# A two-layer attention trunk on one core: a narrower last head, a last head kept on chip, a new entry order

## Chip, cores and metric

The kernel runs as one program on one core of one Trainium2 chip. The metric is the device time of one execution in microseconds (us), median of several runs. Engines are named as in the profile: PE is TensorE (matmuls; PEld is its weight load, which overlaps PE), DVE is VectorE, ACT is ScalarE, POOL is GpSimd, SP is the SyncE queue that issues most transfers.

## What is computed

Two layers on 1024 tokens of width 1024 in float32. Each layer is attention, a residual layer norm, a gated feed-forward part with a width-3 convolution, and again a residual layer norm.

```python
x = layer_norm(alpha * x + mix, ln_g[i, 0], ln_b[i, 0])
ff = conv_ffn(x, ffn_w_in[i], ...)
x = layer_norm(alpha * x + ff, ln_g[i, 1], ln_b[i, 1])

# layer 0: differential attention, 8 heads of 128 columns, two maps per head
a = p[:, :, 0] - lam * p[:, :, 1]          # p = softmax(q k^T - slope * |t - s|)
o = rms_norm(a @ v, subln_g) * (1 - lambda_init);  mix = o @ w_o

# layer 1: neighbourhood attention, 16 heads of 64, grid of 16 rows x 64 columns
s = q_row . k_sel + bias                   # 8 x 16 window around each query
p = softmax(s);  o = p @ v_sel;  mix = o @ w_o + b_o
```

## The kernel before

Every large product is made of three matmuls on rounded parts: a float32 operand is split into a high part (rounded copy, by ACT or POOL) and a low part (operand minus high, by DVE or POOL), and high x high, high x low and low x high are summed in PSUM. `XTh` and `XTl` hold the two parts of the activations, turned, in eight slots of 128x1024; `raw_weights` holds two incoming weight tiles.

The program is a row of stages, each with its own semaphores; at the end of each all engines meet at a barrier and POOL clears the semaphores (line 43): differential attention (prefix `da`), output product with layer norm (`wo`), feed-forward (`ff`), neighbourhood attention (`na`), again `wo`, again `ff`. There is no planner: each engine's list is written out by hand, and semaphores alone tie the lists together.

**Entry (`da`).** PE turns x, then projects head 0: six groups `project(0, j, ...)` of 24 matmuls, in the order of `ORDER`. PE then starts `head(0)`, whose first act is `project(1, 0, 0, 10)`, followed by `score(0, 0)`. `project(1, 0)` needs the split weights of head 1 (`split(1, 0)` on POOL, lines 318 and 320) and all six takes of the projections by ACT (line 595); `score` needs the stacked keys: `KH` and `QS` from ACT (lines 657, 658), their low parts and a copy of `KL` from DVE (lines 758, 761, 764), and a copy of `KH` from POOL (`double_k`, line 344). After these, POOL splits head 1's other weights and only then scales the first map (line 326).

**Last head of `da` and the first `wo`.** Heads 0 and 1 are loaded back and split while the last head runs (`FirstHeads`). The last head's four output pieces go DVE (line 747), `ostage`, SP (line 259), DRAM tensor `heads_t`. The stage ends when the last store has landed. `wo` begins with ACT making the high part of the output weights' row tile 0 (line 1142), DVE its low part (line 1160), then PE's first products (line 1111); heads 2 to 7 are loaded from `heads_t` on the way.

**Neighbourhood attention (`na`).** A head is of 16 steps s (two halves c of 8 query tiles). In a step PE makes the scores of s (lines 2220 to 2227), turns the map of s-2 (line 2236) and weighs the values with the map of s-4 (lines 2264, 2270); between these stand projections of the next head, except in the last head, which has none. DVE adds the bias and takes the minimum (2449), makes the low part of the map (2401), inverts the sum (2459); ACT takes the exponential (2375) and the high part (2328); POOL scales (2108). `V` as the stationary operand holds high and low values side by side (128 columns), the moving operand holds the map's high and low parts side by side, so one matmul of 256 columns gives four partial sums: two in the two halves of the columns, two in the two halves of the partitions. Every second step ACT copies the lower 64 partitions (2343, 64x512), DVE adds them to the upper ones (2415, 64x512) and then adds the two column halves (2422, 64x256) into `ostage`, which SP stores. A query tile whose two grid rows have different windows ("wraps", steps 2 to 5 and 10 to 13) has three matmuls of 256 columns and two of 128 (2 x 64).

**The end.** In the last `ff`, after the last products, DVE handles the eight row tiles t in turn: two adds out of PSUM with sums (1909), mean (977), gain (995), variance (1000), and for t of 4 and more also the last step of the norm, `finish` (1007), one tile behind, with tile 7 at the very end. `finish` needs POOL's root (930). POOL also shifts tiles 0 to 3 (942). SP stores each finished tile of 512 KB (1375).

## Time and profile before

| | |
|---|---|
| median of 3 runs | 2799.16 us (lowest 2797.43) |
| the profiled execution's own time | 2802.47 us |
| its span in the trace | 2800.5 us |
| PE busy | 2658.3 us (95%), 13043 matmuls |
| DVE busy | 1927.1 us (69%) |
| POOL busy | 1671.4 us (60%) |
| ACT busy | 1191.7 us (43%) |
| mean granted PE clock | 0.978 of full |

Busy times are of the whole span. "Idle before" in a row is the engine's idle time just ahead of that instruction, and what follows the arrow is what ended it. PEclk is the clock granted to TensorE: 1.00 is 2.4 GHz and 0.50 is 1.2 GHz. The span and the execution's own time differ by 2.0 us, which lie outside the instructions.

### The profile page before, as it was taken

Reading aid. Unit: us, or ns where it says so; the run is one execution under the profiler, and the core shown is the slowest. Engines: PE = TensorE matmul, PEld = TensorE weight load, DVE = VectorE, ACT = ScalarE, POOL = GpSimd, SP = SyncE. Lnnn points to the kernel's source line nnn. Section 1 sums busy time; section 2 is a strip of 40 time slices with the busy share of each in tenths; the row PEclk is TensorE's granted clock in tenths of the full one; section 3 lists DMA queues with packets and bytes.
Section 4 is the critical chain, followed back from the end, with each engine's and each line's share of the span. In section 5 each row is a group of like instructions: output and inputs, shape, how many; then the busy total and the mean of one; then the engine's idle time right before and its main releaser. Section 6 shows DMA issues by size and latency. Waiting matters only on the chain. (4 is left out here: it accounts for less than half of the span.)

```text
span 2800.5 us, 35855 instructions
## 1 busy us (share of the span) xinstructions
PE 2658.3 (95%) x13043; PEld 2220.2 (79%) x13043; DVE 1927.1 (69%) x2479; ACT 1191.7 (43%) x1785; POOL 1671.4 (60%) x1179
## 2 busy tenths in 40 slices
PE   8999999988899999999989999998788999999998
PEld 6788888877778888888868888887677888888886
DVE  3766667683677766677774777777477777666768
ACT  3455444552253333333344555555415333333333
POOL 4444444333487667777744666655457776677775
PEclk9999999998999999999999999998899999999999
DMA  3010000235011112121222212211411211121212
GB/s 121 21 31 30 30 28 22 64 94 186 15 56 46 46 61 60 46 61 46 63 95 54 56 48 50 47 46 53 156 39 55 60 46 46 59 62 46 60 46 91
DMA packets 214044, 163.83 MB, mean 58 GB/s; under 512 B 36283, under 2 KB 195595, under 8 KB 213899
## 3 DMA queue, kind: packets, MB, share of 16 engines
q1 hardware_dynamic: 213755, 161.38, 19.5%
q8 instruction: 89, 1.46, 0.2%
q10 hardware_dynamic: 144, 0.52, 0.1%
q14 instruction: 56, 0.46, 0.1%
HBM read 137.24 MB, written 24.64 MB: 58 GB/s over the span
## 5 line engine op out<-in xcount | busy, mean ns | idle before, releaser
L1400 POOL TENSOR_TENSOR ff_Rlf<-raw_weights 128x512 f32<-128x512 f32 x210 | 330.6, 1587 | 53.4 <-PE ff_ph L1497 32.6
L1407 POOL TENSOR_TENSOR ff_Rl<-ff_Rlf,ff_Rh 128x512 fp32r<-128x512 f32 x210 | 310.7, 1496 | 25.2 <-ACT ff_Rh L1663 25.2
L1407 POOL TENSOR_TENSOR ff_Rl<-raw_weights,ff_Rh 128x512 fp32r<-128x512 f32 x84 | 157.8, 1888 | 253.5 <-ACT ff_Rh L1663 253.5
L1663 ACT ACTIVATE ff_Rh<-ff_Rlf 128x512 fp32r<-128x512 f32 x210 | 130.5, 630 | 366.6 <-POOL ff_Rlf L1400 366.4
L1497 PE MATMUL ff_ph<-XTh,ff_Rh 128*128 128x512 f32 x672 | 263.2, 392 | 8.7 <-POOL ff_Rl L1407 8.4
L1497 PE MATMUL ff_ph<-XTl,ff_Rh 128*128 128x512 f32 x672 | 262.2, 390 | 0.0
L1497 PE MATMUL ff_ph<-XTh,ff_Rl 128*128 128x512 f32 x672 | 262.1, 390 | 0.0
L1544 PE MATMUL ff_po<-ff_WDh,WH 128*128 128x512 f32 x624 | 244.5, 392 | 0.0
L1544 PE MATMUL ff_po<-ff_WDh,WL 128*128 128x512 f32 x624 | 243.0, 389 | 0.0
L1544 PE MATMUL ff_po<-ff_WDl,WH 128*128 128x512 f32 x624 | 242.9, 389 | 0.0
L1765 DVE TENSOR_TENSOR X<-ff_po,X 128x512 f32<-128x512 f32 x288 | 191.4, 684 | 66.0 <-PE ff_po L1544 66.0
L2108 POOL TENSOR_SCALAR na_E<-na_E,na_rden 128x512 f32<-128x512 f32 x128 | 104.7, 818 | 194.1 <-DVE na_rden L2459 193.5
L689 ACT ACTIVATE da_E<-da_S,da_mn 128x1024 f32<-128x1024 f32 x112 | 125.1, 1117 | 196.4 <-DVE da_mn L769 195.9
L1497 PE MATMUL ff_ph<-WH,ff_Rl 128*128 128x512 f32 x504 | 196.1, 389 | 0.0
L1497 PE MATMUL ff_ph<-WL,ff_Rh 128*128 128x512 f32 x504 | 196.1, 389 | 0.0
L1497 PE MATMUL ff_ph<-WH,ff_Rh 128*128 128x512 f32 x504 | 196.1, 389 | 0.0
L326 POOL TENSOR_SCALAR da_E<-da_E,da_rden,da_neglam 128x1024 f32<-128x1024 f32 x64 | 76.6, 1196 | 199.9 <-DVE da_rden L777 199.7
L1773 DVE SCALAR_TENSOR_TENSOR ff_C<-ff_H,ff_par,ff_C 128x1024 f32<-128x1024 f32 x88 | 158.8, 1804 | 53.8 <-ACT ff_C L1680 52.5
L1779 DVE SCALAR_TENSOR_TENSOR ff_C<-ff_H,ff_par,ff_C 128x1024 f32<-128x1024 f32 x88 | 165.9, 1886 | 1.0
L408 PE MATMUL da_pa<-XTh,da_wh 128*128 128x512 f32 x360 | 150.0, 417 | 9.4 <-POOL da_wl L320 9.4
L769 DVE CUSTOM_DVE_ANT_0 da_S<-da_S,da_strip 128x1024 f32<-128x1024 f32 x128 | 154.0, 1242 | 5.3 <-issue 2.6
L1497 PEld LDWEIGHTS ff_ph<-XTh,ff_Rh 128*128 128x128 f32 x672 | 126.5, 188 | 38.8 <-issue 11.5
(330 smaller groups left out, 7457.6 us busy)
## 6 DMA issues: line engine op xcount, KB each, us to landing
raw_weights<-in_ffn_w_in SPq DMA_DIRECT2D x168, 256.0 KB, 3.3
ff_WDlf<-in_ffn_w_out SPq DMA_DIRECT2D x40, 512.0 KB, 4.0
raw_weights<-in_attn_w_qkv SPq DMA_DIRECT2D x24, 512.0 KB, 3.7
raw_weights<-in_na_w_qkv SPq DMA_DIRECT2D x24, 512.0 KB, 4.2
rpb_rows<-da_rows SPq DMA_DIRECT2D x2, 3840.0 KB, 26.7
na_B<-rpb_rows SPq DMA_DIRECT2D x32, 224.0 KB, 4.4
wo_oraw<-heads_t SPq DMA_DIRECT2D x12, 512.0 KB, 4.6
da_E<-in_x SPq DMA_DIRECT2D x8, 512.0 KB, 6.6
```

What stands on the lines that cost most here:

```text
L408: last = nc.tensor.matmul(out[:], w[:, j // 2, k], x[:, k, t0:t0 + BANK], start=(i == 0), stop=(i == 3 * KT - 1))
L689: nc.scalar.activation(E[:, t % 2, c], Sc[c][:], ACT.Exp, scale=-1.0, bias=mn[:, t % 2, c:c + 1], accum_out=den[:, t % 2, c:c + 1]).then_i ...
L769: nc.vector.tensor_tensor_reduce(out=Sc[c][:], in0=Sc[c][:], in1=strip[:, (QT - 1 - t) * P:(QT - 1 - t) * P + S], scale=1.0, scalar=3.0e38 ...
L1400: nc.gpsimd.tensor_tensor(out=Rf[:, i % SLOTS], in0=quad(*a), in1=quad(*b), op=op).then_inc(quad_sum, 1)
L1407: nc.gpsimd.tensor_tensor(out=Rl[:, i % SLOTS], in0=src, in1=Rh[:, i % SLOTS].bitcast(F32), op=ALU.subtract).then_inc(quad_low, 1)
L1497: last = nc.tensor.matmul(out, w, x[:, k], start=(k == 0 and n == 0), stop=(k == HK - 1 and n == 2))
L1544: last = nc.tensor.matmul(out, a[:, t * P:(t + 1) * P], w[:, half * BANK:(half + 1) * BANK], start=(f == first and j == 0), stop=(f == las ...
L1663: nc.scalar.activation(Rh[:, i % SLOTS], src, ACT.Copy).then_inc(quad_high, 1)
L1765: nc.vector.tensor_tensor(out=at, in0=po[:, r % 4], in1=at, op=ALU.add).then_inc(added, 1)
L1773: nc.vector.scalar_tensor_tensor(out=C[:, parity], in0=H[:, parity, 0:S], scalar=par[:, 1, idx:idx + 1], in1=C[:, parity], op0=ALU.mult, o ...
L1779: nc.vector.scalar_tensor_tensor(out=C[:, parity], in0=H[:, parity, 2:S + 2], scalar=par[:, 3, idx:idx + 1], in1=C[:, parity], op0=ALU.mul ...
L2108: nc.gpsimd.tensor_scalar(E[:, b], E[:, b], rden[:, b:b + 1], 1.0, ALU.mult, ALU.mult).then_inc(scaled, 1)
```

## The change

Five edits; the computed values are the same sums, some in another order.

1. **Entry order.** Group (0, 0) of the projections runs by part (all eight high x high first), so it begins once the turned tokens' and the weight's high parts are there. POOL's copy of `KH` for head 0 moves to ACT (`first_double`); POOL splits head 1's first weights as soon as four groups are done, and the next ones once DVE's copy of `KL` is done.
2. **First output weight ahead.** The high and low parts of the output weights' row tile 0 are made during the last head of each attention and put in slot 5 of `XTh` and `XTl`. `wo` uses them from there for its first four row tiles, and copies them to `wh[:, 0]` and `wl[:, 0]` on ACT and POOL for the others.
3. **Last head stays on chip.** `tail` is slot 6 of `XTl` under another name. The last head's output is written there and split in `wo` (slot 7); it is neither stored nor loaded.
4. **Last `na` head's sum in PSUM.** `weigh_summed` gives the map's high and low parts as separate matmuls that accumulate in the same 128 columns; ACT's copy and DVE's add are 64x256 and the second add is gone.
5. **End.** `finish(4)` moves from tile 5 to tile 6, and the finish and the store of tile 7 are done in two halves.

```diff
 # FirstHeads
+    def weight_high(self, act):
+        self.prefetch.wait(act)
+        self.nc.scalar.activation(self.XTh[:, WEIGHT_SLOT], self.weights, ACT.Copy).then_inc(self.weight_rounded, 1)
+    def weight_low(self, eng, engine):
+        eng.wait_ge(self.weight_rounded, 1)
+        engine.tensor_tensor(out=self.XTl[:, WEIGHT_SLOT], in0=self.weights, in1=self.XTh[:, WEIGHT_SLOT].bitcast(F32),
+                             op=ALU.subtract).then_inc(self.weight_split, 1)
 # diff_attention_stage, SP: the last head
-            head(H - 1, False, False, False)
-            store(H - 1, 2)
-            store(H - 1, 3)
+            head(H - 1, False, False, False, last=True)
...
-                sp.wait_ge(o_stored[b], 16 * 2 * H)
+                sp.wait_ge(o_stored[b], 16 * 2 * (H - 1))
 # POOL
-            double_k(0, (const_set, 2))
-            for j in range(2):
-                split(1, j)
+            split(1, 0)
+            pool.wait_ge(kl_dup, 2)
+            split(1, 1)
 # PE
-                    if j % 2 == 0:
+                    if isinstance(h, int) and h == 0 and j == 0:
+                        pe.wait_ge(w_high, 1)
+                    elif j % 2 == 0:
...
-                    k, p = i // 3, i % 3
+                    k, p = (i % KT, i // KT) if by_part else (i // 3, i % 3)
+                    if by_part and i == KT:
+                        pe.wait_ge(x_low, QT // 2)
+                    if by_part and i == 2 * KT:
+                        pe.wait_ge(w_low, 1)
 # ACT
+            def first_double(c):
+                a, b = slice(c * DH, (c + 1) * DH), slice((1 - c) * DH, (2 - c) * DH)
+                act.wait_ge(stack_high, 2 * c + 1)
+                nc.scalar.activation(KH[b, c], KH[a, c].bitcast(F32), ACT.Copy).then_inc(kh_dup, 1)
...
             stacks(0, False)
+            first_double(0)
             for j in ORDER[5:]:
                 take(0, j)
+            first_double(1)
...
                 ready.high(act, 1)
+                ready.weight_high(act)
                 late_o(o + 3)
 # DVE
                 late_map(QT - 1)
+                ready.weight_low(dve, nc.vector)
                 finish_o(h, 2, late_bank(o + 2))
 # output_stage, ACT
-            for k in range(KT):
+            for k in range(1, KT):
...
+                if k == 1:
+                    nc.scalar.activation(XTh[:, KT - 1], tail[:], ACT.Copy).then_inc(tail_high, 1)
+                    nc.scalar.activation(wh[:, 0], XTh[:, WEIGHT_SLOT].bitcast(F32), ACT.Copy).then_inc(first_copied, 1)
 # output_stage, PE
-                if k == 0:
-                    pe.wait_ge(first_low, 1)
-                else:
+                if k:
                     pe.wait_ge(w_low, k)
 # neighbourhood_stage, POOL (step 10) and ACT (step 9) of the last head
+                    if s == 10 and h + 1 == H:
+                        ready.weight_low(pool, nc.gpsimd)
...
+                    if s == 9 and h + 1 == H:
+                        ready.weight_high(act)
 # PE
+            def weigh_summed(h, s):
+                c, qt = s // QT, s % QT
+                out = pb[(8 * h + s // 2) % 2][:, (s % 2) * P:(s % 2 + 1) * P]
+                p = PT[:, (STEPS * h + s) % 3]
+                v0 = lows[qt] * GW // P
+                whole = range(1, KB) if wraps[qt] else range(KB)
+                for k in whole:
+                    for a in range(2):
+                        last = nc.tensor.matmul(out, V[:, v0 + k, c].rearrange("p a d -> p (a d)"), p[:, k, a],
+                                                start=(k == whole[0] and a == 0),
+                                                stop=(k == KB - 1 and a == 1 and not wraps[qt]))
+                if wraps[qt]:
+                    for r, v in enumerate((V[:, v0, c], Vx[:, qt - WRAP0, c])):
+                        at = slice(r * GW, (r + 1) * GW)
+                        for a in range(2):
+                            last = nc.tensor.matmul(out[:, at], v.rearrange("p a d -> p (a d)"), p[:, 0, a, at], start=False,
+                                                    stop=(r == 1 and a == 1))
 # DVE
+                if h + 1 == H:
+                    at = s % QT // 2 * 2 * P
+                    place = tail[(s // QT) * DH:(s // QT + 1) * DH, at:at + 2 * P]
+                    nc.vector.tensor_tensor(out=place, in0=pb[i % 2][0:DH, 0:2 * P], in1=otmp[:, 0:2 * P],
+                                            op=ALU.add).then_inc(o_out, 1)
+                    return
 # ffn_stage
+        ENDS = {t: [] for t in range(TT)} | ({6: [4, 5], 7: [6, 7]} if last_layer else {5: [4], 6: [5], 7: [6, 7]})
...
-                if t - 1 in FINISHED:
-                    norm.finish(dve, t - 1)
-                if t == TT - 1:
-                    norm.finish(dve, t)
+                for u in ENDS[t]:
+                    if u < TT - 1 or not last_layer:
+                        norm.finish(dve, u)
+                    else:
+                        for half in range(2):
+                            norm.finish_half(dve, u, half)
```

Three places in the program, as lists of instructions in each engine's order (a row is line, operation, output<-inputs, shape, and x with a count of repeats; the line numbers are each kernel's own).

POOL in the entry, before: the splits of head 0's last weights, the two copies of `KH`, the splits of head 1's three weight tiles, the first scaling.

```order
L318 TENSOR_SCALAR da_wh<-raw_weights 128x1024
L320 TENSOR_TENSOR da_wl<-raw_weights,da_wh 128x1024
L344 TENSOR_SCALAR da_KH<-da_KH 64x1024 x2
L318 TENSOR_SCALAR da_wh<-raw_weights 128x1024
L320 TENSOR_TENSOR da_wl<-raw_weights,da_wh 128x1024
L318 TENSOR_SCALAR da_wh<-raw_weights 128x1024
L320 TENSOR_TENSOR da_wl<-raw_weights,da_wh 128x1024
```

And the same place with the change:

```order
L332 TENSOR_SCALAR da_wh<-raw_weights 128x1024
L334 TENSOR_TENSOR da_wl<-raw_weights,da_wh 128x1024
L332 TENSOR_SCALAR da_wh<-raw_weights 128x1024
L334 TENSOR_TENSOR da_wl<-raw_weights,da_wh 128x1024
L332 TENSOR_SCALAR da_wh<-raw_weights 128x1024
L334 TENSOR_TENSOR da_wl<-raw_weights,da_wh 128x1024
```

The copies of `KH` have left POOL; they stand in ACT's list now.

PE at the end of `na` and the start of `wo`, before: turn and weighing of step 15, the weighings of the last two steps, and the first output products.

```order
L2236 MATMUL na_tb<-ident,na_E 128x128 x4
L2264 MATMUL na_pb<-na_PT,na_V 128x256 x3
L2270 MATMUL na_pb<-na_PT,na_V 128x2x64
L2270 MATMUL na_pb<-na_PT,na_Vx 128x2x64
L2264 MATMUL na_pb<-na_PT,na_V 128x256 x8
L1953 UNCONDITIONAL_BRANCH
L1106 UNCONDITIONAL_BRANCH
L1111 MATMUL wo_pg<-WH,XTh 128x512 x2
```

And with the change:

```order
L2303 MATMUL na_tb<-ident,na_E 128x128 x4
L2324 MATMUL na_pb<-na_PT,na_V 128x128 x6
L2331 MATMUL na_pb<-na_PT,na_V 128x64 x2
L2331 MATMUL na_pb<-na_PT,na_Vx 128x64 x2
L2324 MATMUL na_pb<-na_PT,na_V 128x128 x16
L2019 UNCONDITIONAL_BRANCH
L1148 UNCONDITIONAL_BRANCH
L1154 MATMUL wo_pg<-XTh 128x512 x2
```

A weighing of a wrapping tile goes from 5 matmuls to 10, one of another tile from 4 to 8; the first output product reads its weights from `XTh`.

DVE in the last two row tiles of the program, before (from the variance of tile 6 on):

```order
L1000 TENSOR_SCALAR ff_ve<-ff_squares 128x1
L1007 SCALAR_TENSOR_TENSOR X<-ff_C,ff_rstd,WHf_17667 128x1024
L1909 ISA X,ff_sums<-ff_po,X 128x512
L1909 ISA ff_sums 128x1
L1909 ISA X,ff_sums<-ff_po,X 128x512
L1909 ISA ff_sums 128x1
L977 TENSOR_SCALAR ff_negmean<-ff_sums 128x1
L995 SCALAR_TENSOR_TENSOR ff_H<-X,ff_negmean,WHf_17667 128x1024
L1000 TENSOR_SCALAR ff_ve<-ff_squares 128x1
L1007 SCALAR_TENSOR_TENSOR X<-ff_H,ff_rstd,WHf_17667 128x1024 x2
```

And with the change:

```order
L1033 TENSOR_SCALAR ff_ve<-ff_squares 128x1
L1040 SCALAR_TENSOR_TENSOR X<-ff_C,ff_rstd,WHf_17693 128x1024 x2
L1973 ISA X,ff_sums<-ff_po,X 128x512
L1973 ISA ff_sums 128x1
L1973 ISA X,ff_sums<-ff_po,X 128x512
L1973 ISA ff_sums 128x1
L1010 TENSOR_SCALAR ff_negmean<-ff_sums 128x1
L1028 SCALAR_TENSOR_TENSOR ff_H<-X,ff_negmean,WHf_17693 128x1024
L1033 TENSOR_SCALAR ff_ve<-ff_squares 128x1
L1040 SCALAR_TENSOR_TENSOR X<-ff_H,ff_rstd,WHf_17693 128x1024
L1047 SCALAR_TENSOR_TENSOR X<-ff_H,ff_rstd,WHf_17693 128x512 x2
```

Tile 6's turn now carries two finishes (4 and 5) instead of one, tile 5's none, and the last finish is two halves.

## Rows read from the trace of the kernel before

**Rows 1.** The profile's page, part 1: engine, busy us, share, instructions.

```profile
PE 2658.3 (95%) x13043; PEld 2220.2 (79%) x13043; DVE 1927.1 (69%) x2479; ACT 1191.7 (43%) x1785; POOL 1671.4 (60%) x1179
```

**Rows 2.** Timeline, PE, entry: start us, us, engine, line, operation, tiles, shapes, [idle before].

```profile
14.74 0.77 PE L408 MATMUL da_pa<-XTh,da_wh 128*128 128x512 f32 x1 [4.20 <-POOL da_wl L320]
58.69 0.77 PE L408 MATMUL da_pa<-XTh,da_wh 128*128 128x512 f32 x1 [5.24 <-POOL da_wl L320]
```

**Rows 3.** Timeline, POOL, entry.

```profile
11.11 1.05 POOL L318 TENSOR_SCALAR da_wh<-raw_weights 128x1024 fp32r<-128x1024 f32 x1 [7.48 <-DMA raw_weights<-in_attn_w_qkv]
64.79 2.41 POOL L320 TENSOR_TENSOR da_wl<-raw_weights,da_wh 128x1024 fp32r<-128x1024 f32 x1
68.94 1.19 POOL L326 TENSOR_SCALAR da_E<-da_E,da_rden,da_neglam 128x1024 f32<-128x1024 f32 x1 [1.74 <-DVE da_rden L777]
```

**Rows 4.** Timeline, ACT, entry: the last stacked half, the last take.

```profile
51.68 1.04 ACT L658 ACTIVATE da_QS<-da_raw 64x1024 fp32r<-64x1024 f32 x1
53.49 0.60 ACT L595 ACTIVATE da_raw<-da_pb 128x512 f32<-128x512 f32 x1 [0.77 <-PE da_pb L408]
```

**Rows 5.** One line's instructions, DVE: ns min/median/max, first and last start.

```profile
L761 DVE TENSOR_TENSOR da_QS<-da_raw,da_QS x16: 1221/2320/3248, 51.0 to 581.1; 64x1024 fp32r<-64x1024 f32 x16
L764 DVE CAST da_KL<-da_KL x16: 677/684/1529, 52.9 to 582.3; 64x1024 fp32r<-64x1024 f32 x16
```

**Rows 6.** Timeline, end of `da` and start of `wo`.

```profile
649.40 0.42 DVE L747 TENSOR_TENSOR da_ostage<-da_pb,da_og 128x256 f32<-128x256 f32 x1 [3.02 <-PE da_pb L464]
655.44 1.22 PE L1111 MATMUL wo_pg<-WH,XTh 128*128 128x512 f32 x2 [6.08 <-DVE WL L1160]
```

**Rows 7.** Timeline, DVE, first instruction of `ff`.

```profile
763.58 2.29 DVE L1842 TENSOR_TENSOR ff_C<-X 128x2048 f32<-128x2048 f32 x1 [1.10 <-PEq L43]
```

**Rows 8.** Timeline, DVE, one odd step of the last `na` head.

```profile
1968.99 0.68 DVE L2415 TENSOR_TENSOR na_osum<-na_pb,na_otmp 64x512 f32<-64x512 f32 x1 [0.46 <-ACT na_otmp L2343]
1969.71 0.42 DVE L2422 TENSOR_TENSOR na_ostage<-na_osum 64x256 f32<-64x256 f32 x1
1970.05 0.68 DVE L2449 CUSTOM_DVE_ANT_0 na_S<-na_S,na_BI 128x512 f32<-128x512 f32 x1
```

**Rows 9.** Timeline, PEld, last `na` head: weight loads, whose starts pace PE.

```profile
1969.20 0.19 PEld L2226 LDWEIGHTS na_S<-na_KH,na_QZ 128*128 128x128 f32 x1
1969.31 0.19 PEld L2227 LDWEIGHTS na_S<-na_KL,na_QZ 128*128 128x128 f32 x1
1969.83 0.54 PEld L2264 LDWEIGHTS na_pb<-na_PT,na_V 128*128 128x128 f32 x4
```

**Rows 10.** Timeline, PE, last `na` head: turn in step 8, the last two weighings.

```profile
1958.33 1.12 PE L2236 MATMUL na_tb<-ident,na_E 128*128 128x128 f32 x4 [1.02 <-POOL na_E L2108]
1982.61 2.05 PE L2264 MATMUL na_pb<-na_PT,na_V 128*128 128x256 f32 x8 [1.22 <-DVE na_PT L2401]
```

**Rows 11.** Windows: stretch, us, busy (x) of PE, PEld, DVE, ACT, POOL, then PEclk.

```profile
1955.00:1961.00 6.00, 4.98 (x20) 4.13 (x19) 4.27 (x11) 3.38 (x9) 3.90 (x6) 0.50 0.09 22
1962.00:1974.00 12.00, 9.55 (x75) 8.80 (x73) 8.75 (x25) 8.45 (x19) 3.23 (x5) 1.00 0.06 12
655.00:661.00 6.00, 5.56 (x13) 4.40 (x14) 0.39 (x1) 2.07 (x3) 3.24 (x2) 0.50 0.86 305
```

**Rows 12.** Timeline, end of `na` and start of the second `wo`.

```profile
1986.04 0.42 DVE L2422 TENSOR_TENSOR na_ostage<-na_osum 64x256 f32<-64x256 f32 x1
1990.62 3.20 ACTq L1138 DMA_DIRECT2D wo_bias<-in_na_b_o  x1
1996.23 1.22 PE L1111 MATMUL wo_pg<-WH,XTh 128*128 128x512 f32 x2 [11.57 <-DVE WL L1160]
```

**Rows 13.** Timeline, the end: finish of tile 4, POOL's shift, finish of tile 7.

```profile
2783.21 3.34 DVE L1007 SCALAR_TENSOR_TENSOR X<-ff_C,ff_rstd,WHf 128x1024 f32<-128x1024 f32 x1 [0.45 <-POOL ff_rstd L930]
2795.35 1.28 DVE L1007 SCALAR_TENSOR_TENSOR X<-ff_H,ff_rstd,WHf 128x1024 f32<-128x1024 f32 x1 [0.51 <-POOL ff_rstd L930]
2783.08 2.39 POOL L942 TENSOR_TENSOR X<-X,WHf 128x1024 f32<-128x1024 f32 x1
```

More of the change, by code:

```diff
@@ L24 @@
 READY_HEADS = 2
+WEIGHT_SLOT = 5
+TAIL_SLOT = 6
 def hold(eng, sem, value, passed):
@@ L259, in store, with head @@
                 sp.dma_start(OT[bass.ds(h * P, P), q * QW:(q + 1) * QW], ostage[:, q % 2]).then_inc(o_stored[q % 2], 16)
-            def head(h, first, load_two_on, load_three_on):
+            def head(h, first, load_two_on, load_three_on, last=False):
                 if load_two_on:
@@ L269, in head @@
                     load(h + 2, 2)
-                store(h, 0)
+                if not last:
+                    store(h, 0)
                 if load_three_on:
                     load(h + 3, 1)
-                store(h, 1)
+                if not last:
+                    store(h, 1)
             for j in range(3):
```

114 lines of the change are left out of this document (75 added, 39 removed).

## The prediction

> **What bounds the kernel now.** I read the page first: PE is busy 95% of the span, the next engine 69% [rows 1]. Between the stages, though, PE waits, and the chain of waits at those places names other engines. So the change is priced place by place: how long PE (or, at the very end, DVE) waits there, what is last to arrive, and what is last with the change. None of the edits touches the feed-forward parts or the steady heads, which hold most of the span; what it can win is the sum of a few waits.
>
> The places: PE waits 4.20 us for POOL's first low part and 5.24 us for head 1's [rows 2]; 6.08 us between the first attention and its output product [rows 6]; 11.57 us at the second such place [rows 12]; in the last neighbourhood head, which has no projections, DVE and ACT set the step and PE idles (9.55 us busy of 12 at full clock) [rows 11]; at the end DVE finishes after PE.
>
> **Entry.** Group (0, 0) can start once POOL's first high part is there: 11.11 + 1.05 = 12.16, with the hand-over 12.3, not 14.74 [rows 2, 3]. Its low parts are wanted eight and sixteen products later, after they are done. The six groups follow one another, so ACT's stacking ends 2.45 earlier, at 52.72 - 2.45 = 50.3 [rows 4]. Then ACT makes one copy of `KH` (1.05, like the stacks beside it) and the last take (0.60): 52.0 [rows 4]. PE needs that take and starts head 1's projection at 52.0, not 58.69 [rows 2]; its weights are no longer late, since POOL splits them during the projections. DVE starts when the first of four stacked copies is done, 50.3 - 3 x 1.0 = 47.2, and needs twice 1.22 + 1.22 + 0.68 without POOL beside it [rows 5]: 53.5. POOL then does two splits of 1.05 + 2.41 with hand-overs of 0.3 and 0.1 [rows 3]: 53.5 + 2 x 3.85 = 61.2, and only then scales the first map, which happened at 68.94 before [rows 3]. The map itself would be ready nearer to 59.3: PE is 6.7 earlier and its ten products now run at full clock (512 columns at 2.4 GHz are 0.21, at 1.2 GHz 0.43, and it idled before them), which is 2 more, less a small wait for DVE's 53.5. So POOL is what is late next, by 2. Gain 68.94 - 61.2 = **7.7**; bounds 5 (DVE and POOL collide as in the 3.25 that line 761 reached [rows 5]) and 9.3 (POOL not late).
>
> Why collisions matter: at the end of the program a finish that takes 1.28 alone took 3.34 while POOL's shift ran [rows 13]. The Trainium skill, "SBUF — State Buffer", section "SBUF: two separate sides", says that DVE and GpSimd share a port pair by an exclusive lock, held for the whole instruction, and that DVE asks for it in certain modes or with two SBUF inputs; by that rule the new low part on POOL in step 10 costs DVE nothing, since DVE's operations there take one input from PSUM. If it did hold DVE up, the price would be one operation of 2.41, which the range holds.
>
> **First attention to output product.** DVE's last finish ends at 649.82 [rows 6]. Before, the store, the barrier, ACT's high part and DVE's low part followed; now only the barrier, 1.1 (the idle time at another change of stage [rows 7]): 650.95 instead of 655.44. Gain **4.5**. The two new operations fit into idle time: DVE waits 3.02 before its last finish alone [rows 6], ACT and POOL have no other work there. PE starts at half clock before as well (0.50 in 655 to 661 [rows 11]); how long it stays so may shift the gain by 1.5 either way.
>
> **Last neighbourhood head.** In an odd step DVE stands 0.46 for ACT's copy, adds (0.68) and adds again (0.42): from 1968.53 to 1970.05, 1.52 [rows 8]. With 256 instead of 512 elements the add is like the second one, 0.42, and the wait perhaps 0.25: 0.67, so 0.85 less (0.64 if the wait stays). Six odd steps have it, 5 to 15. In 5 and 7 it is hidden: PE's turn at 1958.33 waits for POOL [rows 10], whose table work the change leaves. That leaves four, 3.4, of which ACT takes back some 0.4 each in steps 9 and 13, where a copy of 1.05 stands between two exponentials. The last pair also loses the second add, which ran against POOL.
>
> PE's side is what speaks against it. A weighing has 8 or 10 products instead of 4 or 5: 8 x 4 + 8 x 5 = 72 more. No row shows a 128-column product of this kind; each has its own weight load, and these start 0.11 apart for 64 columns and (0.54 - 0.19) / 3 = 0.12 for 256 [rows 9]. So I price one at 0.11 at full clock and 0.21 at half: a weighing goes from 0.5 to 0.9. The Trainium skill, "TensorE: Matmul & The Clock Gate", section "Back-to-back issue gap", gives about 81 ns for a stream of 128-column products with their loads; no run shows it here, and by it a weighing would be 0.65 and the end of the head some 0.5 earlier, an estimate of 2773.5 for the whole. At 0.11 a pair of steps costs PE about 4.0 to 4.5, against DVE's 4.9 - 0.85 = 4.1: at full clock PE just keeps up. At half clock it doesn't: the last two weighings took 2.05 for 8 products [rows 10] and would take 3.4. Full clock throughout: I follow the list to an end of DVE's and POOL's work at about 1981.5, 5.0 before 1986.46 [rows 12]. Half clock as in 1955 to 1961 and at the tail [rows 11]: 1.2 or less. I take 3.3.
>
> The store is gone as well: the second `wo` began at about 1990.3, just ahead of ACT's issue at 1990.62 [rows 12]; 3.85 after DVE's end, of which 1.1 is barrier [rows 7]: 2.7. Head together **6.0**.
>
> **Second output product.** PE began 5.9 after the stage did (1996.23 [rows 12]), behind the bias transfer that ACT issues (3.20), a high and a low part. Now it begins with the stage. But row tile 1's low part still comes behind that issue, at 3.5 + 1.05 + 0.1 + 2.4 = 7.1, and PE's first 24 products last 5.2 at full clock and up to 10 at half. So between 3 and 5.7 is kept: **4.5**. Later row tiles were ahead of PE before; the new wait of ACT for `first_used` comes only at tile 5.
>
> **The end.** Before, tile 6's adds waited behind finish(4), 2783.21 to 2786.55 [rows 13]. Now DVE goes on to tile 6 and is held by PE's half tiles instead, then does finishes 4 and 5 together (2 x 1.28): tile 7's last finish ends 1.7 earlier, and the last transfer is half as long, 0.6. Gain **2.3**; bounds 1 and 3.
>
> **Sum.** 7.7 + 4.5 + 6.0 + 4.5 + 2.3 = 25.0. The profiled execution took 2802.5 (span 2800.5 and 2.0 around it), so it would give 2777.5; the median of the runs is 3.3 below it, 2799.2: 2799.2 - 25.0 = **2774.2**.
>
> **Rivals.**
> - *PE bound at half clock in the last head.* Its clock was at half in half of that head [rows 11], and products have doubled. [...] Against: PE has more to do there, and its clock was full from 1962 to 1974 with a fifth idle. A pair of steps at half clock is some 7 for PE against 4.9 before; three such pairs cost 6 and the head's gain is gone: 25.0 - 6 = 19, with the tail 15: 2780 to 2784. Chance 0.2.
> - *Entry wait replaced.* POOL's two splits after DVE's copy, or ACT's copies ahead of the take, hold the first map longer: gain 3 instead of 7.7: 2779. For it: POOL is already the latest in my sum. Chance 0.1.
> - *Slower than before.* One mechanism: narrow products that add into the same columns cost far more than a load. There are 144 in that head; to eat the 19 of the other places and the head's own 6 each must cost 0.17 more than 0.11, 0.28, all on PE's path. Time from 2799 up. Even half-clock rows stay at 0.21 to 0.23. Chance 0.02.
> - *The gain is handed back*, since transfers or norms in `wo` set the pace there: what is won at both starts (9) is lost: 2783. Against: right after such a start PE is busy 5.56 of 6 us [rows 11], so it, not the transfers, sets the pace. Chance 0.05.
>
> **How the numbers follow.** The forecast has 0.63, own range 2768 to 2779 from the terms' bounds. The range to 2786 takes in the first, second and fourth rival; below, all upper bounds (9.3, 6, 7.7, 5.7, 3) add up to 31.7, which gives 2767.5, and the spread of the runs before (2797.43 to 2799.16) takes it to 2766. A measurement of this kernel tells about 2% from no change, which is 56 us. None of the cases reaches that on either side: faster 0.01, same 0.98, slower 0.01.
>
> **What would show it.** Entry: PE's first 512-column product near 12.3, head 1's first near 52, POOL's first scaling near 61.2, with the low clock ahead of head 0 gone. Starts of `wo`: PE's wait 1.5 to 2 instead of 6.1, and about 2 instead of 11.6. Last head: four bias operations from step 9 on 0.85 closer per pair; PEld steps of 0.11. End: DVE with no finish between tiles 5 and 6. Wrong would be: a first scaling after 65, a longer stretch of PEclk 0.50 in the last head, or a wait of PE inside `wo` that was not there.

## The result and the profile after

| | before | after |
|---|---|---|
| median of 15 runs each | 2800.78 us | 2770.12 us |
| ratio | | 0.9902, 95% interval 0.9887 to 0.9917 |
| the profiled execution | 2802.47 us | 2771.33 us |
| its span | 2800.5 us | 2769.5 us |

The predicted time was 2774.2, the difference measured is 30.7 us instead of 25.0. Under 2%, as forecast. But the 15 runs are of two kinds: thirteen between 2766.5 and 2775.5, and two at 2786.6 and 2790.8. Seven more runs of the same kernel, in a later set, gave three at 2767.3 to 2771.8 and four at 2790.4 to 2792.2. So of 22 runs 16 lie at 2770.3 (mean) and 6 at 2790.6, and nothing lies between. The long ones have a mean granted clock of 0.976 or 0.977, the others 0.983 to 0.987; the profile shown here is not of a long one. The kernel before had no second kind: its 53 runs, those of the later sets included, lie between 2797.4 and 2804.4 (one disturbed run of 4436.9 apart). This second kind turned out to be the most instructive part of the case.

The page of the changed kernel, part 1 (columns as in [rows 1]):

```profile
PE 2657.3 (96%) x13115; PEld 2222.4 (80%) x13115; DVE 1915.0 (69%) x2471; ACT 1192.6 (43%) x1789; POOL 1670.3 (60%) x1180
```

PE is busy for the same time as before although it has 72 more products; what went is its idle time. Where, is read by laying the same points of both traces beside each other: how much earlier each comes, and what the stretch since the last point gave.

| point | before | after | gained in the stretch | predicted |
|---|---|---|---|---|
| DVE's last finish of the first attention ends | 649.82 | 640.55 | 9.3 | 7.7 |
| PE's first output product | 655.44 | 641.73 | 4.4 | 4.5 |
| PE turns `V` in the last `na` head | 1943.12 | 1928.00 | 1.4 | 0 |
| DVE's last add of that head ends | 1986.46 | 1965.97 | 5.4 | 3.3 |
| PE's first output product, second time | 1996.23 | 1967.01 | 8.7 | 7.2, of the two rows |
| first product of the second `ff` | 2106.95 | 2078.39 | -0.7 | |
| mean of row tile 5, last norm | 2780.15 | 2751.21 | 0.4 | 0 |
| end of the span | 2800.5 | 2769.5 | 2.1 | 2.3 |

How far one profile can be trusted is shown by a second one of the changed kernel, of an execution that took 2767.3 (**f4_after_again**, below). There the first attention ends at 637.99, a gain of 11.8 instead of 9.3, and the stretch up to the turn of `V` gives 2.9 instead of 1.4; the two starts of `wo`, the last head and the end come out within 0.1. The first attention holds 29.5 us of half clock before, 21.1 in the table's profile and 12.3 in this one.

The entry, timeline of the changed kernel (start us, us, engine, line, operation, tiles, shapes, [idle before]); PE, ACT and POOL rows answer to [rows 2 to 4]:

```profile
11.48 2.08 PE L429 MATMUL da_pa<-XTh,da_wh 128*128 128x512 f32 x8 [1.38 <-POOL da_wh L332]
49.09 0.47 PE L429 MATMUL da_pa<-XTh,da_wh 128*128 128x512 f32 x1 [1.12 <-ACT da_raw L616]
...
48.35 0.60 ACT L616 ACTIVATE da_raw<-da_pb 128x512 f32<-128x512 f32 x1
...
50.70 1.06 POOL L332 TENSOR_SCALAR da_wh<-raw_weights 128x1024 fp32r<-128x1024 f32 x1 [9.90 <-DVE da_KL L796]
55.68 2.39 POOL L334 TENSOR_TENSOR da_wl<-raw_weights,da_wh 128x1024 fp32r<-128x1024 f32 x1
58.06 1.19 POOL L340 TENSOR_SCALAR da_E<-da_E,da_rden,da_neglam 128x1024 f32<-128x1024 f32 x1
```

The order of things is the forecast's: PE starts with POOL's high part, head 1 waits for ACT's last take and no longer for weights, POOL comes to the first map straight from its second split. Eight products in 2.08 us is full clock from the start.

The two starts of `wo`, and the last head's end, which answer to [rows 6, 7, 12]:

```profile
640.13 0.42 DVE L779 TENSOR_TENSOR last_head<-da_pb,da_og 128x256 f32<-128x256 f32 x1 [2.58 <-PE da_pb L485]
641.73 0.77 PE L1154 MATMUL wo_pg<-XTh 128*128 128x512 f32 x1 [1.64 <-PEq L45]
...
1965.55 0.42 DVE L2507 TENSOR_TENSOR last_head<-na_pb,na_otmp 64x256 f32<-64x256 f32 x1 [1.52 <-ACT na_otmp L2432]
1966.97 0.38 ACTq L1185 DMA_DIRECT2D wo_bias<-in_na_b_o  x1
1967.01 0.69 PE L1154 MATMUL wo_pg<-XTh 128*128 128x512 f32 x2 [1.91 <-PEq L45]
```

Both times only the barrier stands between DVE's last operation and PE's first: 1.18 and 1.04. The issue of the bias transfer, 3.20 before [rows 12], takes 0.38 here.

The last head in windows (us, busy (x) of PE, PEld, DVE, ACT, POOL, then PEclk), to be read against [rows 11]:

```profile
1938.00:1948.00 10.00, 8.72 (x69) 8.00 (x69) 6.51 (x19) 5.80 (x14) 6.69 (x10) 1.00 0.01 2
1948.00:1958.00 10.00, 10.00 (x83) 9.64 (x82) 7.65 (x21) 8.01 (x18) 5.20 (x6) 1.00 0.00 0
1958.00:1966.00 8.00, 6.86 (x59) 6.44 (x57) 4.72 (x11) 5.08 (x11) 6.04 (x4) 1.00 0.01 3
```

PE went from 80% busy to 10.00 of 10 us in the middle of the head, at full clock from 1933.4 on (the first 5.4 us of the head, with the turn of `V`, are at half). And the end, to be read against [rows 13]:

```profile
2757.61 2.46 DVE L1040 SCALAR_TENSOR_TENSOR X<-ff_C,ff_rstd,WHf 128x1024 f32<-128x1024 f32 x2
2764.73 1.42 DVE L1047 SCALAR_TENSOR_TENSOR X<-ff_H,ff_rstd,WHf 128x512 f32<-128x512 f32 x2 [0.51 <-POOL ff_rstd L963]
```

The two finishes stand together, 2.46 for both, no longer beside POOL's shift.

### The profile page after: what moved, and what is told of

The parts are those of the page before. It is cut to its first block and busy times, and to the rows that moved or that the text cites. A ratio compares the mean times of both kernels' runs of the same rounds, so it can differ in the third digit from the quotient of the medians.

```text
span 2769.5 us, 35973 instructions
## 1 busy us (share of the span) xinstructions
PE 2657.3 (96%) x13115; PEld 2222.4 (80%) x13115; DVE 1915.0 (69%) x2471; ACT 1192.6 (43%) x1789; POOL 1670.3 (60%) x1180
## 5 line engine op out<-in xcount | busy, mean ns | idle before, releaser
L769 DVE SCALAR_TENSOR_TENSOR da_E<-da_E,da_rden 128x1024 f32<-128x1024 f32 x64 | 95.9, 1499 | 81.9 <-POOL da_E L340 81.9
```

Of the source, the lines that this page charges most:

```text
L769: nc.vector.scalar_tensor_tensor(out=E[:, b, 0], in0=E[:, b, 0], scalar=rden[:, b, 0:1], in1=E[:, b, 1], op0=ALU.mult, op1=ALU.add).then_i ...
```

## The experiments

All ratios are against runs of the kernel before on the same chip. "The head" is the stretch from PE's turn of `V` to the end of DVE's last add: 43.34 before, 37.97 after.

### The last head taken apart

Theory: DVE's and ACT's shorter operations and PE's clock each have a share in the head's gain. Rivals: one of them is all of it, or the gain has nothing to do with the products.

**e1_wide_head**, edit 4 undone:

```diff
-                if h + 1 == H:
-                    return weigh_summed(h, s)
...
-                n = 2 * P if h + 1 == H else 4 * P
+                n = 4 * P
...
+                    nc.vector.tensor_tensor(out=place.rearrange("p (t q) -> p t q", t=2), in0=osum[:, :, 0], in1=osum[:, :, 1],
+                                            op=ALU.add).then_inc(o_ready, 1)
```

> The changed kernel with its edit 4 undone: 256-column products, 64x512 copy and add, second add (into the tail). Measured from PE's turn of V (1928.00 in the trace of the changed kernel, 1943.12 before) to the end of DVE's last add of the head: 37.97 in the changed kernel, 43.34 before. Theory (the narrower operations and the clock that stays full make the head's 5.4): 42.5 to 43.5 here, half clock in part of the head again, time 2770.1 + 5 = 2775. Rival (the head is shorter because output stays on chip and nothing is stored): 38 to 39 here and 2771.

The head took 41.89, just under the expected 42.5, with the clock at half for 14.6 us of it (19.3 before, 5.4 in the changed kernel); four runs at 2772.5 to 2776.3, median 2772.8, ratio 0.9897 (0.9880 to 0.9913). The profiled run is the longest of the four. So edit 4 is worth 3.9 in the head of the profiles and 2.7 in the medians, and 1.5 of the 5.4 came to this head without it. The rival that it is worth nothing falls.

**e2_narrow_pe_full_adds** and **e3_wide_pe_narrow_adds**: one side of edit 4 each.

```diff
 # e2: PE narrow, ACT and DVE as long as before
+                n = 4 * P
...
+                    nc.vector.tensor_tensor(out=place, in0=one, in1=one, op=ALU.max).then_inc(o_ready, 1)
 # e3: PE wide, ACT and DVE 64x256
-                if h + 1 == H:
-                    return weigh_summed(h, s)
```

> The changed kernel with the narrow products on PE, but ACT's copy and DVE's add at 64x512 again and a second operation of 64x256 on DVE, as before (the second operation takes a maximum of one block with itself, so the values are the same). Theory A (DVE's and ACT's shorter operations give about 3.4 of the head's 5.4 and the fuller PE, by keeping its clock at full, about 2): clock full through the head, from the turn of V to DVE's last add 41 to 41.5. Theory B (the clock is the whole of it): 38 to 39. Theory C (the shorter operations are the whole of it; the doubled products cost what the clock gives): 43 to 44.

> The changed kernel with the wide products of before on PE, but ACT's copy and DVE's add at 64x256. Half of the last head's sums are left out of the output. Theory A (both count): PE idles more, its clock falls to half somewhere in the head, 39.5 to 41.5 from the turn of V to DVE's last add. Theory B (the clock is the whole of it): 43. Theory C (the shorter operations are the whole of it, the narrow products only cost PE): 36.5 to 38, shorter than the changed kernel's 37.97.

e3 (whose output lacks half of the last head's sums) took 37.99 in the head, as long as the changed kernel, with the wide products on PE and 3.4 us of half clock beside the usual stretch at its start; four runs at 2769.5 to 2772.3, median 2770.3. So with the shorter operations of ACT and DVE alone the whole 3.9 is there; theory A is out by its own number, theory C's range held at its edge. That PE is fuller gives nothing. Between e1 and e3 the half clock in the head also went from 14.6 to 8.6 us, and no run parts what of the 3.9 is this and what is the operations themselves.

e2 fitted none of the three in its profile: that run took 57.79 in the head and 2787.17 in all. Its other four runs, 2773.0 to 2775.3, are on average 3.9 above the changed kernel's 2770.1, so without the shorter operations the narrow products gain nothing there either; no trace shows their head. In the profiled run the clock was at half from 1935.7 to 1986.9, and until 1978 PE was busy 6.00 of every 6 us of it:

```profile
1942.00:1948.00 6.00, 6.00 (x27) 5.61 (x26) 2.60 (x8) 2.82 (x7) 1.38 (x2) 0.50 0.00 0
1948.00:1954.00 6.00, 6.00 (x29) 5.91 (x29) 2.79 (x8) 2.21 (x6) 3.02 (x2) 0.50 0.00 0
```

**e4_before_narrow**: the kernel before with edit 4 alone, `weigh_summed` as in the change and one add into `ostage`.

> The kernel before with edit 4 alone (narrow products, one add, still into ostage and stored). Theory: the head's 5.4 come without the other edits: 2800.8 - 5.4 = 2795.4, from the turn of V to the last add 38 instead of 43.34. Rival (the edit needs the stage without stores or the shift of the clock's phases that the entry brings): 42 to 43.3 and 2800.

The head took 38.84, 4.5 less than before; nine runs at 2793.9 to 2799.5 and one at 2815.3, median 2796.8, ratio 0.9993 (0.9977 to 1.0008). The trace has the gain without the other edits, and the median is 4.0 below that of the kernel before beside it; the interval of the ratio, which takes in the long run, still includes 1, so the runs alone do not show the gain. The long run is there too, with a mean clock of 0.972 where the other nine have 0.978 to 0.981.

### The entry, and the first weight

**e5_old_entry**, **e6_by_part_only**, **e7_order_only**: edit 1 undone whole, its second half undone, its first half undone.

```diff
 # e5 and e6
-            split(1, 0)
-            pool.wait_ge(kl_dup, 2)
-            split(1, 1)
+            double_k(0, (const_set, 2))
+            for j in range(2):
+                split(1, j)
...
-            first_double(0)
-            first_double(1)
 # e5 and e7
-                by_part = isinstance(h, int) and h == 0 and j == 0
+                by_part = False
```

> The changed kernel with edit 1 undone whole (group (0, 0) in the old order, KH copied by POOL ahead of the splits). Theory: the entry is worth 8.8 to 9.2 and touches nothing else: first scaling at 68.9, first output product of the first attention at 650.5 instead of 641.7, time 2770.1 + 9 = 2779. Rival (part of the 9 comes back, since the clock and the transfers settle in the eight heads anyway): 2773 to 2775. A second expectation for every kernel with the narrow products: about one run in eight is 14 to 20 longer, at a mean clock of 0.976 to 0.978 instead of 0.985.

> The changed kernel with only the first half of edit 1: group (0, 0) by part, but POOL's copies and splits in the old order. Theory (start and order are in series): first product at 11.5, projections end near 48, no half clock in them; POOL then does two copies and two splits, first scaling at about 63.4, time 2770.1 + 5 = 2775. Rival A (POOL's order is all that counts, the early start is absorbed): scaling at 68, 2779. Rival B (the early start is all): 58 to 59, 2770.

> The changed kernel with only the second half of edit 1: the new order on POOL and ACT, but group (0, 0) starts when all its parts are there. Theory: first product at 14.7, then half clock in the first projections as before (steps of 0.43 up to 19.5), projections end at 53.4, head 1's first product at 54.6, first scaling at 63.5, time 2770.1 + 5 = 2775. Rival (the half clock there comes from something else than the late start): projections end near 51.2, 3.3 later than in the changed kernel and no more, scaling at 61.3, 2773.

| | first product | projections end | first scaling | ninth reciprocal | runs, us |
|---|---|---|---|---|---|
| neither (e5) | 13.97 | 52.04 | 67.33 | 141.54 | 2800.6, 2796.9, 2802.7, 2798.7 |
| by part (e6) | 11.65 | 48.14 | 64.03 | 136.52 | 2778.3, 2772.5, 2795.6, 2792.7 |
| order (e7) | 13.88 | 51.98 | 62.07 | 134.62 | 2774.7, 2776.6, 2791.5, 2792.2 |
| both (after) | 11.48 | 47.97 | 58.06 | 132.21 | 16 at 2770.3, 6 at 2790.6 |

At the ninth reciprocal, one head on, by part alone gives 5.0, the order alone 6.9, both 9.3. Both rivals that one half is all of it fall. These numbers hold to about 2 us only: profiles with one and the same entry have this point at 130.9 and 132.2 (the changed kernel twice), or at 141.5 and 139.6 (e5 and f2 below), depending on where a stretch of half clock falls.

By part wins 4.0 at the end of the projections from 2.4 at their start: the rest is the clock, at half from 14.6 to 18.0 in e7 and not at all in the projections of e6. This stretch follows the late start in the kernel before, e4, e5 and e7, but not always: f2 starts at 13.91 as well, runs at full clock from there and ends its projections at 50.40 instead of 52.04.

In e6 PE stands for POOL's low part for 5.24 again, as in [rows 2], and POOL then for the reciprocal:

```profile
53.37 0.77 PE L429 MATMUL da_pa<-XTh,da_wh 128*128 128x512 f32 x1 [5.24 <-POOL da_wl L334]
64.03 1.20 POOL L340 TENSOR_SCALAR da_E<-da_E,da_rden,da_neglam 128x1024 f32<-128x1024 f32 x1 [2.16 <-DVE da_rden L807]
```

The times do not follow the entries. e5 (median 2799.7) lost 29.6, not 9: in all four of its runs the mean clock was 0.974 to 0.976. Its head took 60.15 us, and the clock was at half from 1925.7 to 2000.8:

```profile
1945.00:1955.00 10.00, 10.00 (x43) 9.10 (x43) 5.14 (x14) 3.47 (x11) 5.17 (x7) 0.50 0.01 2
1955.00:1965.00 10.00, 10.00 (x45) 9.61 (x45) 4.44 (x11) 5.12 (x11) 1.50 (x3) 0.50 0.00 0
1965.00:1975.00 10.00, 10.00 (x45) 9.74 (x45) 3.98 (x10) 2.92 (x7) 4.29 (x4) 0.50 0.00 0
```

Half as many products per window as in the changed kernel's 1948 to 1958, with PE, DVE and ACT doing the same work in the same order. The longer runs of e6 and e7 carry a mean clock like it, 0.975 to 0.978. A run whose last head stays at half clock to its end is called held from here on. Three profiles show one (e2, e5, e8); the others are counted as held by their time and mean clock.

**e8_first_weight_in_stage**, edit 2 undone:

```diff
-                ready.weight_high(act)
-                ready.weight_low(dve, nc.vector)
...
+            nc.scalar.activation(XTh[:, WEIGHT_SLOT], raw[:, 0], ACT.Copy).then_inc(first_high, 1)
+            dve.wait_ge(first_high, 1)
+            nc.vector.tensor_tensor(out=XTl[:, WEIGHT_SLOT], in0=raw[:, 0], in1=XTh[:, WEIGHT_SLOT].bitcast(F32),
+                                    op=ALU.subtract).then_inc(first_low, 1)
```

> The changed kernel with edit 2 undone: the first output weight's high part is made by ACT and its low part by DVE at the start of each output stage, as before; the last head still stays on chip. Theory: PE waits 1.04 + 1.22 and two hand-overs longer at the first start, 1.64 + 2.4 = 4.0; at the second also behind the bias transfer's 3.2: 1.9 + 5.6 = 7.5. Of the second, little is kept apart from it, so the two output stages end 2.4 and 5 later and the time is 2770.1 + 7.4 = 2777.5; the last heads are 0.3 shorter without the weight's two parts. Rival (row tile 1's low part sets the pace anyway): PE waits 2 after its first products of the changed kernel, and only 3 in all is lost, 2773.

PE's wait at the first start was 3.98, forecast 4.0; at the second it was 4.67, forecast 7.5, since the issue of the bias transfer took 0.38 and not 3.2:

```profile
643.93 1.22 PE L1156 MATMUL wo_pg<-XTh 128*128 128x512 f32 x2 [3.98 <-DVE XTl L1219]
```

Of it 3.4 is still there when the last head turns `V`, and the second output stage is 3.6 longer from the last add to the first product of `ff`; three runs at 2776.2 to 2777.4, one, the profiled, at 2798.1 with a held head of 56.7. Edit 2 is worth 7.0 in the trace and 7.1 in the times (2777.2 for the three against 2770.1); the rival said 3. That the sum came out right (2777.5 expected) with a wait 2.8 too long in it is in part luck.

### What holds the clock

The narrow weighing needs as many weight loads as products. Loads of six products, first the changed kernel at full clock, then e5 at half (a PEld row's second number spans all six):

```profile
1958.22 0.75 PEld L2324 LDWEIGHTS na_pb<-na_PT,na_V 128*128 128x128 f32 x6
...
```

```profile
1958.37 1.40 PEld L2320 LDWEIGHTS na_pb<-na_PT,na_V 128*128 128x128 f32 x6
```

That is 0.11 and 0.21 apart; at full clock it is the spacing of [rows 9] where a product has 64 columns as well as where it has 256. At half clock a head of such products takes PE so long that DVE and ACT wait for it instead of the other way round. The theory to be tried: the head is held because its products are narrow, and with more columns in each of as many products it is not. Rival: any head that PE bounds is held.

The Trainium skill, "TensorE: Matmul & The Clock Gate", section "What's actually happening", says that activity releases the throttle, and its table there gives full clock to a PE that is busy. By the profile's busy share this case does not agree: 10.00 of 10 us at half clock, window after window from 1945 to 1985 and 9.00 of 9 up to 1994. The Trainium skill also warns on this page, in the section "Seeing it yourself", that the clock's trace events have been observed to be unreliable and that the clock has been seen stuck for over 50 us, at a setting that it writes K=1/4. The setting is another here, a granted clock of 0.50 for 75 us, and it is real: the weight loads are 0.21 apart instead of 0.11, and the run is some 20 us longer.

**f4_after_again**, **f1_dense**, **f2_dense_old_entry** put the theory and the rival apart: as many products and loads, but each product streams its 128 columns twice, into two halves of the bank; the sums are the same, and ACT and DVE read as many elements, in two pieces.

```diff
-                        last = nc.tensor.matmul(out, V[:, v0 + k, c].rearrange("p a d -> p (a d)"), p[:, k, a],
+                        last = nc.tensor.matmul(out, V[:, v0 + k, c].rearrange("p a d -> p (a d)"),
+                                                p[:, k, a].unsqueeze(1).to_broadcast([P, 2, P]),
...
```

> The changed kernel itself, beside the next two, to count how often its last neighbourhood head runs at half clock from end to end. Theory (seen so far in the kernels with narrow products: the old entry 4 of 4 runs, each half of the new entry alone 2 of 4, the changed kernel 2 of 15): most runs at 2767 to 2776 with a mean clock of 0.983 to 0.987, and about one in eight at 2786 to 2791 with 0.976 or 0.977. Rival (the two long runs were a disturbance of that chip): none here.

> The changed kernel with as many products in the last head, each of which streams its 128 columns twice, into both halves of the step's 256 columns of the bank (the 64-column ones likewise to 2 x 64), so that either half holds the sum; ACT and DVE still read one half, 64x256. A product's own weight load paces it at 0.11 at full clock and 0.21 at half, which 256 columns fit into. Theory (what holds the clock at half is that a product of 128 columns fills only part of such a slot): the head lasts about 38 from the turn of V to the last add as in the changed kernel, no run is held at half clock, time 2768 to 2773 in all runs. Rival A (any head that PE bounds stays at half clock): long runs as often as in the changed kernel. Rival B (256 columns from a repeated operand cost more than a slot): the head lasts 41 or more at full clock and the time is 2774 or more.

> The old entry (as in e5_old_entry, where 4 of 4 runs had the last head at half clock and took 2797 to 2803) with the doubled columns. Theory: no run is held at half clock; the head lasts 38 to 40 instead of 60.15, the time is 2770.1 + 7 to 9, 2777 to 2779. Rival A (the phase that the entry leaves decides, whatever the products stream): 2797 to 2803 again.

| | entry | head in the profile | runs, us |
|---|---|---|---|
| f4, narrow | new | 37.99 | 2767.3, 2790.4, 2770.6, 2791.9, 2791.5, 2771.8, 2792.2 |
| f1, doubled | new | 38.45 | 2771.3, 2771.1, 2773.0, 2772.8 |
| e5, narrow | old | 60.15 | 2800.6, 2796.9, 2802.7, 2798.7 |
| f2, doubled | old | 38.44 | 2779.2, 2781.2, 2780.9, 2780.5 |

Ratios: f4 0.9942 (0.9917 to 0.9966), f1 0.9897 (0.9882 to 0.9911), f2 0.9927 (0.9913 to 0.9942), e5 0.9993 (0.9979 to 1.0007). The old entry is the sharpest pair, held in four of four, with the doubled columns in none, though e5 and f2 ran on different chips; f4, beside f1 and f2 on one chip, was held in four of seven and they in none of eight. Over the whole record narrow products were held in 17 of 53 runs (6 of 22 of the changed kernel, 1 of 5 of e2, 1 of 10 of e4, 4 of 4, 2 of 4, 2 of 4 and 1 of 4 of e5 to e8), the doubled ones with f3 in none of 12, the wide ones of e1, e3 and the kernel before in none. Windows of f2 in its head, to be read against e5's above:

```profile
1945.00:1955.00 10.00, 8.41 (x64) 7.68 (x64) 6.43 (x17) 5.66 (x15) 6.66 (x10) 1.00 0.01 2
1955.00:1965.00 10.00, 10.00 (x83) 9.78 (x83) 7.96 (x20) 7.82 (x16) 5.67 (x6) 1.00 0.00 0
```

PE bounds this head as well (10.00 of 10), and it is not held: the rival falls. In the old entry twice the columns make the head not longer but 21.7 shorter. At full clock they cost little: the head is 0.5 longer than the changed kernel's. f2's median of 2780.7 lies above the expected 2777 to 2779; it is 8.6 above f1's, as much as the old entry was said to cost (7 to 9).

What decides, in one kernel, which runs are held is open. The stretch in which PE turns `V` is at half clock in every profile here (1919.8 to 1933.4 in the changed kernel), and there are two ways into a held head. In e5 the clock did not rise as the weighings began and stayed down. In e2 and e8 it rose there as in the changed kernel, was full for 6.8 us and fell again. Nor does a late rise mean a held head: in e4, e6 and e7 the narrow weighings also began at half clock, and 7.8 to 8.0 us later it rose. Up to that point PE's work is the same: in one window e6 (first row, not held) and e5 (second row, held) both have 37 products, without a gap:

```profile
1939.00:1947.00 8.00, 8.00 (x37) 7.61 (x35) 4.87 (x13) 3.15 (x8) 5.18 (x6) 0.50 0.07 16
1939.00:1947.00 8.00, 8.00 (x37) 7.61 (x35) 5.10 (x14) 3.02 (x7) 4.94 (x6) 0.50 0.07 16
```

The time at which the head begins does not tell either: the older entries put the turn of `V` 2.7 to 6.7 us later and are held more often, but e2's held head begins at 1923.8, 4.2 earlier than the changed kernel's. In these runs the number of columns tells whether the head can be held; what makes it so in one run and not in the next, none of them shows.

### A version built from this

**f3_dense_better**: the doubled columns, POOL's third split of head 1 moved behind the first scaling, and the bias transfer issued behind ACT's copies.

```diff
-                    if t == 0 and split_last:
+                    if t == (1 if first else 0) and split_last:
```

> The kernel with doubled columns (2772.0) and two more edits, each at a place where the changed kernel still waits. In the entry POOL scales the first map ahead of head 1's third weight split (the map's reciprocal was there at 56.7, POOL came to it at 58.1); at the second output product ACT issues the bias transfer behind its copies instead of ahead of them (3.2 of ACT's queue). Theory (both waits are on PE's path): first scaling at 57.0, PE's second scores 1.0 earlier and the heads after them too (the ninth reciprocal at 131.4 instead of 132.4), the second output stage 0.6 shorter, the first feed-forward product of layer 1 at 112.6 after the last add instead of 114; all runs unheld, 2770.3. Rival (POOL's third split then stands in the second map's way, and DVE's and POOL's operations collide elsewhere): 132.4 and 2772 as in the kernel without the two.

Four runs at 2768.9 to 2774.3, median 2770.6, ratio 0.9888 (0.9872 to 0.9905): the changed kernel's better kind of run, in every run. Four runs alone would not show this; with f1 and f2 it is none held of 12. The first scaling came at 56.99 as expected, 1.1 earlier, but one head on the ninth reciprocal was at 131.90 instead of the expected 131.4, 0.3 before the changed kernel's, since DVE's operation behind it met POOL's split:

```profile
56.99 1.20 POOL L340 TENSOR_SCALAR da_E<-da_E,da_rden,da_neglam 128x1024 f32<-128x1024 f32 x1 [2.80 <-DVE da_rden L809]
58.23 2.05 DVE L769 SCALAR_TENSOR_TENSOR da_E<-da_E,da_rden 128x1024 f32<-128x1024 f32 x1 [1.55 <-POOL da_E L340]
59.29 3.22 POOL L334 TENSOR_TENSOR da_wl<-raw_weights,da_wh 128x1024 fp32r<-128x1024 f32 x1
```

1.29 and 2.40 became 2.05 and 3.22. The bias edit is not told apart: the output stage took 112.0 from last add to the first product of `ff`, against 112.4 in the changed kernel and 114.3 in f1, where PE ran at full clock at the start and then stood 2.01 for DVE. There was little to win: the expectation counted 3.2 for the issue, which is the kernel before; in the changed kernel it took 0.38.

## Why the prediction was right, and where not

- **Entry, 7.7 forecast, 9.3 measured, at its upper bound** (11.8, beyond it, in the second profile). The chain was right link by link: first product 11.5 for 12.3 (of this 0.8 the data had simply landed earlier; between 13.9 and 14.7 in the old order too), head 1 at 49.1 for 52.0, scaling at 58.1 for 61.2. The mis-sized step is "the six groups follow one another, so ACT's stacking ends 2.45 earlier": the projections ended 5.5 earlier, because in this profile of the kernel before the late start was followed by a stretch at half clock, up to 19.5. I had put that stretch's end into a sentence on what would be seen, and not into the sum. The sum of e6 and e7 apart (11.9) is more than both together; that POOL becomes the latest would do this, but the 2 us by which such a point moves from profile to profile would too.
- **First start of `wo`, 4.5 forecast, 4.4 measured**, and a wait of 3.98 against 4.0 in the experiment that undid it.
- **Last head, 3.3 forecast, 5.4 measured.** The term was built on DVE's step ("0.85 less"), and the experiments say that this is the right place: the 3.9 are there with the shorter operations, wide products or narrow. The 3.3 was a choice between 5.0 (full clock throughout) and 1.2 (half clock as before), and the clock was full from the first weighings on; that it is not in every run is the rival below. 1.5 came to this head without edit 4, with 14.6 us of half clock in it instead of 19.3. PE's price of 0.11 a product at full clock and 0.21 at half was right; the 81 ns that the prediction set beside it are not what this head has (and 2774.2 less 0.5 is 2773.7, not 2773.5). POOL's new low part in step 10 cost DVE nothing, as forecast: DVE's operations beside it took what they take elsewhere (0.69 for this one, again at 1955.35 with POOL idle).

```profile
1950.72 2.38 POOL L107 TENSOR_TENSOR XTl<-raw_weights,XTh 128x1024 fp32r<-128x1024 f32 x1
1951.03 0.69 DVE L2492 TENSOR_TENSOR na_PT<-na_tb,na_PT 128x512 fp32r<-128x512 f32 x1 [0.36 <-ACT na_PT L2416]
```

- **The store, 2.7 forecast, 2.9 measured.**
- **Second start, 4.5 forecast, 5.2 kept** (5.9 at the start, 0.7 handed back). The step that failed is "row tile 1's low part still comes behind that issue": the issue took 0.38.
- **End, 2.3 forecast, 2.1 measured.**
- **1.8 in stages that no edit touches** had no term in the sum. 1.4 of it lies between the first output product and the turn of `V`, where the half clock went from 35.0 to 33.7 us; that is worth 0.7 at most, and the rest is open.
- **The rival "PE bound at half clock in the last head"** was given 0.2 and 2780 to 2784. It happened in 6 of 22 runs, near to its chance; its price was the worst number in the text. The 7 for a pair of steps was near (3.84, 4.44, 4.07, 4.07, 4.07, 3.47 and 3.84 a step in e2's head), but I took three such pairs, because I thought that full work brings the full clock back. In a held head nearly all steps last that long, and the head 57 to 60 instead of 38: 2790.6, outside the range of 2766 to 2786. The argument "against: PE has more to do there" does not hold: PE was busy 10.00 of 10 us in window after window, and the clock stayed at half.
- The rivals "entry wait replaced" and "the gain is handed back" did not come (0.7 of the second start was handed back); 0.28 a narrow product did not come either.

The gain was 5.7 more than forecast (30.7 for 25.0), and the time 4.1 below the number: the other 1.6 is the start of the sum, a median of 2799.2 from three runs, which is 2800.8 over fifteen. The mean of all 22 runs (2775.9) came out 1.7 above the number.

That the time lies within the range of 2766 to 2786 is in part luck. The terms of the sum and their mechanisms held, but the chance by which a run is held was not in them (the first rival had it, at too low a price): two of the first 15 runs were, four of the seven later ones, and the median of those seven is 2790.4, above the range. The sum treated the clock as a spread of 1 or 2 us in each term, where it is also a case of its own that costs 20. The sum's own range, 2768 to 2779, also took the lower bounds less than in full: 5, 3, 1.2 + 2.7, 3 and 1 add up to 15.9, which is 2783.

## What to carry to other kernels

Where products are made smaller, look not only at what one costs at full clock but at what the engine does when it is at half: if it is then the one that all wait for, the clock may stay there, as it did with products of 128 columns and not with 256. A median of a few runs does not show this; look at the mean clock of each run, and give a rare, dear case its own price. And where a half-clock stretch stands behind a wait, ask what goes with the wait: in the entry, 2.4 us of it took a stretch worth another 1.6 along, though f2 shows the same wait without the stretch.

## What the runs showed of the hardware

- PE busy 10.00 of 10 us with the granted clock at 0.50, for 49 us on end (the half clock itself lasted 75; e5, 1945 to 1994), in a head of mostly 128-column products; with each of them streamed twice (f2) the same head was at full clock from 1940.7 on. Narrow products were held in 17 of 53 runs, doubled ones in none of 12.
- A 256-column product whose moving operand is the same 128 columns read twice starts every 0.117 at full clock (f1, eight loads in 1.01), against 0.111 for 128 columns (the changed kernel, eight in 0.97).
- The issue of one transfer on ACT's queue (`wo_bias`) took 3.20 in the kernel before and 2.91 in e4, the two that store the last head just ahead of it; in the kernels that do not it took 0.38, in three of them (e5, e6, f2) 0.81 to 1.12. No run singles out the cause.
- In three places a two-input operation of DVE and one of POOL, both with all their inputs in SBUF, fell together, and the second to start ended about as late as if it had waited for the first: in the changed kernel DVE's 1.22 took 2.91, to 1.08 after the end of POOL's 2.37, and in [rows 13] 3.34, to 1.08 after the end of POOL's 2.39. In f3 DVE's 1.29 took 2.05 beside POOL's high part (58.15, 1.06), and POOL's low part behind it, 2.40 alone, took 3.22.
